# Loading an expert's weights as six 2 MB pieces from a copy laid out by the launch, instead of twelve 1 MB pieces

## The reference: one layer of a hybrid trunk, ending in a mixture of experts

```python
logits = (x2 @ w_router) + b_router
top_v, top_i = lax.top_k(logits, TOP_K)            # 4 of 32 experts a row
gates = jax.nn.softmax(top_v, axis=-1)
def expert_block(args):                            # a block of rows that share one expert e
    xb, e = args
    gu = xb @ w_gu[e] + b_gu[e]                    # (1024 x 2048)
    gate = jnp.minimum(gu[:, :D_FF], SWIGLU_LIMIT)
    up = jnp.clip(gu[:, D_FF:], -SWIGLU_LIMIT, SWIGLU_LIMIT)
    hid = (up + 1.0) * gate * jax.nn.sigmoid(SWIGLU_ALPHA * gate)
    return hid @ w_dn[e] + b_dn[e]                 # (1024 x 1024)
# each row adds its four results, weighted by its gates; residual; final RMSNorm
```

## Time and profile before

| what | value |
|---|---|
| median of three runs | 1675.86 us (1673.62 to 1677.0) |
| the profiled execution (its time is shown as its span) | 1674.4 us |
| PE busy | 1529.6 us (91%) |
| gate/up loads | 256 of 1024 KB, 16.4 us median from issue to landing |
| down loads | 128 of 1024 KB, 14.6 us median |
| bytes moved by DMA | 478.17 MB |
| DMA queue of SP | 69.7% of 16 engines' span |
| HBM read | 472.06 MB |

### The profile page before, as it was taken

One profiled execution on the slowest core, in us unless ns is written; L12 is line 12 of the kernel. 1 busy time (PEld: TensorE's weight loads), 2 busy tenths in 40 slices (PEclk: granted clock), 3 DMA queues, 4 the chain that ended last, 5 costly groups with the idle time before them and its releaser, 6 DMA issues.

```text
span 1674.4 us, 20671 instructions
## 1 busy us (share of the span) xinstructions
PE 1529.6 (91%) x7178; PEld 703.5 (42%) x7179; DVE 354.8 (21%) x859; ACT 348.2 (21%) x672; POOL 125.6 (8%) x232
## 2 busy tenths in 40 slices
PE   8999999999999998887899988788999887998994
PEld 6676666666665433222233332222333222332331
DVE  2655422334211521010011010100111010101015
ACT  3535423534100211111111111101111110111111
POOL 0200000000000010000001000000101000010010
PEclk9999999999999999898999999889999997999996
DMA  7221232212464379999989899999899999579897
GB/s 262 92 79 57 95 109 78 76 51 101 139 237 166 134 288 409 416 419 407 417 311 415 353 415 417 412 411 421 312 368 393 412 414 402 215 309 411 324 409 265
DMA packets 92698, 478.17 MB, mean 286 GB/s; under 512 B 13096, under 2 KB 17053, under 8 KB 43507
## 3 DMA queue, kind: packets, MB, share of 16 engines
q1 hardware_dynamic: 84168, 461.47, 69.7%
q0 software_dynamic: 8096, 16.04, 2.9%
q10 hardware_dynamic: 394, 0.15, 0.0%
HBM read 472.06 MB, written 15.51 MB: 291 GB/s over the span
## 4 chain that ended last, share of the span: by engine, by line
PE 73%; DMA 18%; DVE 4%; issue 3%; SPq 1%; ACT 1%; ACTq 0%; DVEq 0%; POOLq 0%; POOL 0%
PE bank L613 28%; PE bank L1040 21%; DMA ring<-in_w_gate_up 17%; PE bank L1066 17%; PE bank L617 3%; PE bank L1046 1%; DVE r_kv L1494 1%; DVE r_v L1497 1%; PE bank L889 1%; DVE r_c L1497 1%; SPq L567 0%; PE bank L764 0%; DVE r_qk L1491 0%; SPq L574 0%; PE bank L884 0%
## 5 line engine op out<-in xcount | busy, mean ns | idle before, releaser
L1040 PE MATMUL bank<-ring,r_kv 128*64 128x512 f32 x2184 | 519.6, 623 | 89.7 <-DMA ring<-in_w_gate_up 89.0
L1040 PEld LDWEIGHTS bank<-ring,r_kv 128*64 128x64 f32 x2184 | 156.6, 142 | 397.7 <-issue 302.1
L1066 PE MATMUL bank<-ring,r_kv 128*64 128x512 f32 x1248 | 292.2, 612 | 0.7 <-ACT r_kv L1150 0.7
L613 PE MATMUL bank<-r_xt,ring 128*128 128x336 f32 x848 | 249.1, 448 | 1.1 <-ACT r_o L1150 0.9
L1491 DVE TENSOR_SCALAR r_kv<-bank 128x512 f32<-128x512 f32 (+1 forms) x80 | 55.0, 687 | 919.4 <-PE bank L1046 917.9
L613 PEld LDWEIGHTS bank<-r_xt,ring 128*128 128x128 f32 x848 | 158.1, 190 | 78.0 <-issue 5.6
L1066 PEld LDWEIGHTS bank<-ring,r_kv 128*64 128x64 f32 x1248 | 93.3, 144 | 198.2 <-issue 197.3
L1150 ACT ACTIVATE r_xt<-bank 128x512 f32<-128x512 f32 x39 | 23.3, 597 | 511.8 <-PE bank L1066 511.8
L1437 ACT ACTIVATE r_o<-r_kv 128x512 f32<-128x512 f32 x39 | 24.6, 631 | 318.2 <-DVE r_kv L1491 318.2
L617 PEld LDWEIGHTS bank<-const,r_v 64*128 64x128 f32 (+3 forms) x524 | 50.0, 157 | 77.2 <-DVE r_v L1497 43.9
L617 PE MATMUL bank<-const,r_v 64*128 64x64 f32 (+3 forms) x524 | 64.4, 259 | 10.6 <-DVE r_v L1497 10.4
(11 more groups left out here) (257 smaller groups left out, 958.2 us busy)
## 6 DMA issues: line engine op xcount, KB each, us to landing
ring<-in_w_gate_up SPq DMA_DIRECT2D x256, 1024.0 KB, 16.4
ring<-in_w_down SPq DMA_DIRECT2D x128, 1024.0 KB, 14.6
ring<-in_w_in SPq DMA_DIRECT2D x12, 2048.0 KB, 8.0
ring<-in_w_proj_b SPq DMA_DIRECT2D x2, 2048.0 KB, 7.8
ring<-in_w_proj_a SPq DMA_DIRECT2D x2, 2048.0 KB, 9.7
ring<-in_w_out SPq DMA_DIRECT2D x2, 2048.0 KB, 8.0
ring<-y_rows SPq DMA_DIRECT2D x8, 512.0 KB, 9.1
ring<-in_w_uq SPq DMA_DIRECT2D x2, 1152.0 KB, 9.2
```

Of the source, the lines that this page charges most:

```text
L613: ins = pe.matmul(out, l, r, start=(n == 0), stop=(n == len(pairs) - 1), **kw)
L1040: ins = pe.matmul(half(gate_bank if q < 2 else up_bank, q % 2), xg[:, k, :], w[:, 512 * q:512 * q + 512], start=False, stop=False, skip_gr ...
L1066: ins = pe.matmul(half(out_bank, t), hidT[:, 2 * (j % 2) + s, BLK * h:BLK * h + BLK], w[:, s, 512 * t:512 * t + 512], start=(j == 0 and s ...
```

## The change: six pieces of 2 MB

The launch adds two inputs to the program, `in_w_gate_up_t` and `in_w_down_t`, and drops the two original ones. They hold the same values in another order: for each expert, four gate/up pieces and two down pieces, each piece 128 partitions of 4096 values (`SLOT`), that is 16 KB in a run and 2 MB contiguous. A piece is what fills one slot of `ring`: up(0) and up(1) together, up(2) and up(3), and so on. The places in SBUF, the matmuls and their order stay as they are.

SP issues six loads to an expert instead of twelve. A load waits until both its parts are used. TensorE waits for a load once, ahead of the first of its two parts: that is ahead of the even numbers.

```diff
-        up_in = [sem(f"up_in{n}") for n in range(8)]
-        dn_in = [sem(f"dn_in{n}") for n in range(4)]
+        up_in = [sem(f"up_in{n}") for n in range(4)]
+        dn_in = [sem(f"dn_in{n}") for n in range(2)]
...
-        gu = i["w_gate_up"][0].rearrange("e (k p) f -> p e k f", p=128)
-        dn = i["w_down"][0].rearrange("e (j p s) f -> p e j (s f)", p=128, s=2)
+        gu = i["w_gate_up_t"].rearrange("e n p f -> n p e f")
+        dn = i["w_down_t"].rearrange("e n p f -> n p e f")
+
+        def up_home(n):
+            return pslot(UPSLOT[n], SLOT)
+
+        def dn_home(n):
+            return pslot(DNSLOT[n], SLOT)
...
             with sp.Fori(1, NE) as e:
                 before = sp.value_load(firsti[0:1, bass.ds(e, 1)].bitcast(I32), min_val=0, max_val=MAXB)
-                for k in range(8):
-                    sp.wait_ge(m_up, before * 8 + k + 1)
-                    sp.dma_start(up_w(k), gu[:, bass.ds(e, 1), k, :].rearrange("p a f -> p (a f)")
-                                 ).then_inc(up_in[k], 16)
-                for j in range(4):
-                    sp.wait_ge(m_down, before * 4 + j + 1)
-                    sp.dma_start(dn_w(j).rearrange("p s f -> p (s f)"),
-                                 dn[:, bass.ds(e, 1), j, :].rearrange("p a f -> p (a f)")).then_inc(dn_in[j], 16)
+                for n in range(4):
+                    sp.wait_ge(m_up, before * 8 + 2 * n + 2)
+                    sp.dma_start(up_home(n), gu[n, :, bass.ds(e, 1), :].rearrange("p a f -> p (a f)")
+                                 ).then_inc(up_in[n], 16)
+                for n in range(2):
+                    sp.wait_ge(m_down, before * 4 + 2 * n + 2)
+                    sp.dma_start(dn_home(n), dn[n, :, bass.ds(e, 1), :].rearrange("p a f -> p (a f)")
+                                 ).then_inc(dn_in[n], 16)
...
             def gate_up(k, e):
 
-                pe.wait_ge(up_in[k], 16 * e + 16)
+                if k % 2 == 0:
+                    pe.wait_ge(up_in[k // 2], 16 * e + 16)
...
             def down(j, e):
 
-                pe.wait_ge(dn_in[j], 16 * e + 16)
+                if j % 2 == 0:
+                    pe.wait_ge(dn_in[j // 2], 16 * e + 16)
...
+    arrays["in_w_gate_up_t"] = np.ascontiguousarray(np.asarray(inputs["w_gate_up"])[0].reshape(
+        NE, 4, 2, 128, 2 * D).transpose(0, 1, 3, 2, 4).reshape(NE, 4, 128, SLOT))
+    arrays["in_w_down_t"] = np.ascontiguousarray(np.asarray(inputs["w_down"])[0].reshape(
+        NE, 2, 2, 128, 2 * D).transpose(0, 1, 3, 2, 4).reshape(NE, 2, 128, SLOT))
```

More of the change, by code:

```diff
@@ L546, in _ @@
             sp.dma_start(bd_rows, i["b_down"][0]).then_inc(ld_late, 16)
-            for k in range(4):
-                sp.dma_start(up_w(k), gu[:, 0, k, :]).then_inc(up_in[k], 16)
+            for n in range(2):
+                sp.dma_start(up_home(n), gu[n, :, 0, :]).then_inc(up_in[n], 16)
             filled(sp, "g", 3)
@@ L558, in _ @@
             filled(sp, "ya", 7)
-            for k in range(4, 8):
-                sp.dma_start(up_w(k), gu[:, 0, k, :]).then_inc(up_in[k], 16)
+            for n in range(2, 4):
+                sp.dma_start(up_home(n), gu[n, :, 0, :]).then_inc(up_in[n], 16)
             filled(sp, "out", 2, 0)
             filled(sp, "out", 2, 1)
-            for j in range(4):
-                sp.dma_start(dn_w(j).rearrange("p s f -> p (s f)"), dn[:, 0, j, :]).then_inc(dn_in[j], 16)
+            for n in range(2):
+                sp.dma_start(dn_home(n), dn[n, :, 0, :]).then_inc(dn_in[n], 16)
             sp.wait_ge(moe_tab, 1)
@@ L2067 @@
        "g_q_norm", "g_kv_norm", "w_uq", "w_uk", "w_uv", "w_proj_b", "w_out", "g_ffn_norm", "w_router", "b_router",
[L2068 removed]
+       "b_gate_up", "b_down", "g_final_norm"]
 OUTS = [("y_p", (1, TX, D)), ("y_s", (1, TS, D)), ("p_lat", (1, 1, TP, KVL)), ("p_kr", (1, 1, TP, ROPE)),
```

## The result

The changed kernel takes 1690.46 us (median of 4 runs, 1689.17 to 1694.06) against 1676.14 us for the kernel before in the same comparison: a ratio of 1.0089, 95% interval 1.0072 to 1.0105. The forecast was 1686 us, slower by 10 us; it is slower by 14.3. In the two profiled executions the span grows from 1674.4 to 1689.4 us, by 15.0.

What follows compares the result with a forecast made beforehand. In the expert stage DMA was taken to bound four paced stretches, TensorE the others. 9.8 + 2.8 + 3.4 - 6.0 = +10.0 us on the median 1675.9 gave 1686 us, range 1677 to 1698.

Steps and rivals of the forecast that it cites:

- Term 1: End of each of four paced stretches: first matmuls wait for the whole 2 MB, 2.45 us later each, 9.8 us.
- Term 2: Restart after a dry place: the second 2 MB load lands 0.7 us late, 4 x 0.7 = 2.8 us.
- At each of them several MB stand in the queue: At the other late issues, down loads included, a filled queue keeps DMA from stopping: no cost.
- Term 3: Unpaced experts with loads just in time: new short TensorE waits at 10, 20 and 31, together 3.4 us.
- if the waits at unpaced experts [...] make TensorE's clock fall: Sign of being wrong: short waits at unpaced experts lower TensorE's clock, for which the forecast took nothing.
- its 5 us for the clock: Allowance outside the sum: if short waits also lower TensorE's clock, 3 x 1.7 = 5 us more.
- Term 4: Paced stretches, 598 us of loads: runs of 16 KB raise DMA's rate by 1.0%, -6.0 us.
- The estimate by the overhead of a packet: Alternative for the rate in paced stretches: three cycles of overhead per packet give a 0.6% gain, 3.5 us.
- fewer transfers save fixed costs: Rival on the weight loads: six transfers less per expert give back fixed costs, 4% or 24 us, 1668 us; chance 0.08.
- The rule that the prediction takes: About 2.0 us plus bytes / 436e9 per DMA, 53 against 41 us per expert; held not to apply to a full queue.
- the long runs hold up the small transfers: Rival: scatters delayed to 10.4 to 12.8 us among longer packets, or slower rate; 1708 us or above; chance 0.06.

Runs made afterwards that it cites:

- pair_wait: Kernel before, but TensorE waits ahead of each even part for both loads of the slot, SP issuing as before: 1687.09 us, 1.0064.
- late_release: Kernel before with its 1 MB loads, but SP issues both loads of a slot only when both its parts are used: 1682.3 us, 1.0037.
- late_dn: Kernel before, but SP issues both down loads of a slot only when both parts are used, gate/up loads as before: 1679.09 us, 1.0023.
- coarse_8k: Changed kernel's six 2 MB loads and waits, but from the old layout in runs of 8 KB: 1702.26 us, 1.0155 to the kernel before.
- first_slot_fine: Changed kernel, first slot as two separate 1 MB loads: 1678.81 us, 1.0015; its twin with old layout and 8 KB runs throughout: 1683.52 us, 1.0037.
- late_up: Kernel before, but SP issues both gate/up loads of a slot only when both parts are used, down loads as before: 1679.48 us, 1.0029.
- the two single experiments: late_release and pair_wait, each one half of the coarse grain on the kernel before: +6.2 and +10.7 us, 16.9 together.
- first_eighth_split: first_slot_fine (new layout) with the first eighth as two 512 KB halves, waited for one by one: 1672.76 us, 0.9987 to the kernel before.
- before_split: Kernel before, old layout, with only the first eighth in two 512 KB halves, waited for one by one: 1673.6 us, 0.9985.
- fine_t: Kernel before with its twelve 1 MB loads and waits, but reading the new layout in 8 KB runs at 16 KB distance: 1674.84 us, 0.9996.

## Why the prediction was right, and which terms were not

The direction, the places and the kinds of loss are those of the prediction, and 14.3 us lie within its range. Its sum of 10.0 came closer than its terms did: the sizes measured below, about 9, 6, 9 and -7 us, sum to 17, so some of the nearness is luck.

*Term 1, the whole piece at the end of a paced stretch, 9.8 us.* Right. `pair_wait` has this and the short waits alone: 10.7 us, interval 7.5 to 13.9; the short waits are 1.6 of it in its trace.

*Term 2, the restart, 2.8 us.* Mechanism right, size wrong: 6.2 us (3.7 to 8.5) by `late_release`, and 4 x 1.7 = 6.9 by the landings in the two traces. Two steps failed. A lone 2 MB takes 7.7 us, not 7.35; the page of the kernel before had such a row, two 2 MB loads of `in_w_proj_b` that land 7.8 us after issue. And "At each of them several MB stand in the queue (a load 16 us old on landing), so DMA never stops" was read from a row of a paced block and applied to all; behind a dry place the queue had 1.3 us in hand, and `late_dn` shows a queue run empty, and 3.9 us of cost (1.0 to 6.7) where I had put nothing.

*Term 3, the short waits, 3.4 us.* Too small. Places: the waits at experts 10, 20 and 31 came as forecast, and those at 12, 22 and 28, put at nothing, came too, with one more at expert 2 (24 waits), since the restart was later. Size: 8.6 us in the three pieces of this trace where 3.4 were forecast. The wait at expert 10 was as forecast (1.25 us for 1.2) and left the clock up. Those at experts 20 and 31 came to 1.83 and 1.96 us where 1.2 and 1.0 were forecast, and the clock fell, for which I had taken nothing; together that makes 3.6 us of 1.8. This is one of the signs that the prediction named for being wrong ("if the waits at unpaced experts [...] make TensorE's clock fall"). With its 5 us for the clock the term reaches 8.4, just short of the 8.6. In the trace of `coarse_8k` the same three pieces cost 4.5 us, so the term varies from one execution or kernel to the next.

*Term 4, the rate, -6.0 us.* The rate itself is as forecast: 419 against 414 GB/s, 1.2%, for an extrapolated 1.0%. Its worth was 3.7 us between the two `first_slot_fine` kernels (1 to 7) and 11 between the two coarse ones (7 to 15); 1.2% of the 598 us that DMA paces are 7. The estimate by the overhead of a packet (the Trainium skill, DMA: Bandwidth & Descriptors, "Why small descriptors are slow") was 0.6%, and the slope between two rows was nearer. The sum by that estimate is 9.8 + 2.8 + 3.4 - 3.5 = 12.5, against 10.0; the prediction has 12.7 and 10.2 there, which is a slip.

*The rivals.* That fewer transfers save fixed costs is out: with half as many transfers and the old runs, `coarse_8k` has the old rate in a paced stretch, 415 GB/s for 414. The rule that the prediction takes from the same page of the Trainium skill ("Anatomy of one DMA"), about 2.0 us to each transfer beside its bytes, is given there for transfers that GpSimd issues; these are SP's. In these traces a fixed part shows only where a load meets an empty queue, and even there not twice for two loads. Behind the dry places one load of 2 MB lands after 7.7 us, while in `late_release` and `late_up` two loads of 1 MB, the second issued 0.6 us behind the first, are complete after 7.2 to 7.8 us. That the long runs hold up the small transfers is half right: a scatter takes longer, but no wait of TensorE on it appeared. After, all 39 scatters:

```profile
DMA to landing us min/median/max: 2.8/8.0/8.4
```

against 6.6 at the median in the earlier trace rows. It is the long runs that do it, not the large loads: in `coarse_8k` the median is 6.6 us again.

*Open:* where the 9 us between the sum of the two single experiments and `coarse_8k` lie; why a late release of the down slots alone costs 3.9 us; why halving the first eighth gives 2.5 us and not 5, and why its gain seems gone with two slots fine. Differences of 2 us are at the limit of these intervals. The best of all these kernels, `first_eighth_split`, is 0.13% faster than the kernel before, an interval that just excludes no change; `before_split` reaches the same without the copy by the launch.

## What to carry to other kernels

A transfer that is merged with its neighbour is later twice: it starts when the last part is free and is usable when the last byte is there. In a stretch that the transfers pace this costs nothing to each, and once, at the end, the time of the part that was added; so keep the piece small that the first waiting instruction needs. Merging behind it won back most of the loss here, but no kernel here is clearly faster for it: `first_slot_fine` is at 1.0015, and `before_split`, which merges nothing, is as good as the best that merges. Whether a later issue is covered has to be read at the place where the queue is shortest, behind the stage in which the engine is the slower one: compare the time to landing there with that of a load alone.

## What the runs showed of the hardware

A run of 16 KB in HBM goes out as one packet (24615 packets of at least 8 KB where 24576 runs were asked for). Loads with such runs move at 417 to 419 GB/s in a paced stretch, in five kernels, and loads with runs of 8 KB at 413 to 415, in nine, whether they are of 1 or 2 MB. Beside loads with runs of 16 KB a scatter of 64 rows lands after 8.0 us at the median instead of 6.6. On an empty queue a load of 1 MB lands in 4.7 to 5.0 us (5.1 to 5.4 in `fine_t`, where it takes 8 KB out of every row of 16), one of 2 MB in 7.7 with runs of 16 KB and in 7.4 to 7.6 with runs of 8 KB (`coarse_8k`), and two of 1 MB issued together are both there after 7.2 to 7.8: the longer run shows no gain in a load alone.

TensorE's granted clock stayed at 1.00 over the eight matmuls behind waits of up to 1.36 us in the kernel after, and stood at 0.52 to 0.63 behind waits of 1.77 to 1.96 us. In other kernels 1.39 us at the start of a block brought it down, 1.59 us there did not, and 1.81 us in the middle of a run of matmuls did not either. So the length of the last wait alone does not decide.
